# An attention encoder layer on eight cores: VectorE's chain behind each attention unit in two parts, V tiles by weight slices, the gate stage in three blocks

## What is computed

```python
a = rms_norm(h, g_mix); z = a @ w_in                     # q, k, v, u, v_gmlp
q, k = apply_partial_rope(q), apply_partial_rope(k)       # 16 of 64 dims
# differential attention, 8 heads, two softmaxes each
pr = softmax(q k^T * 64**-0.5); o = (pr[0] - lam * pr[1]) @ v
attn_out = rms_norm(o, g_subln) * (1 - lambda_init)       # per head
gmlp_out = gelu(u) * (w_spatial @ layer_norm(gelu(v_gmlp)) + b)   # chunks of 128 tokens
h = h + concat(attn_out, gmlp_out) @ w_out                # 2048 x 2048
h = h + conv_glu_ffn(rms_norm(h, g_ffn))                  # d_ff 5632, conv width 3
gate = sigmoid(rms_norm(h, g_ple) @ w_ple_gate)
h = h + (p @ w_ple_up) * gate
return rms_norm(h, g_final)
```

## Time and profile before

| | |
|---|---|
| median of 3 runs | 2027.28 us (2026.97 to 2114.86) |
| profiled execution | 2025.8 us; span of its slowest core, core 4: 2024.0 us |
| spans of the eight cores | 2012.2 to 2024.0 us |
| TensorE matmul busy | 1900.0 us, 94% |
| VectorE, ScalarE, GpSimd busy | 995.8 us (49%), 736.8 us (36%), 185.2 us (9%) |
| chain that ended last | TensorE 81%, VectorE 8%, issue 4%, ScalarE 3%, DMA 3% |
| stages of core 4, us from the start of the span | loads and K projection to 125, V to 235, attention 450 to 890, output projection's rest to 945, feed-forward to 1867, gate stage to 2009, last writes |

### The profile page before, as it was taken

One profiled execution on the slowest core, in us unless ns is written; L12 is line 12 of the kernel. 1 busy time (PEld: TensorE's weight loads), 2 busy tenths in 40 slices (PEclk: granted clock), 3 DMA queues, 4 the chain that ended last, 5 costly groups with the idle time before them and its releaser, 6 DMA issues.

```text
span 2024.0 us, 31135 instructions; the slowest of 8 cores (2012.2 to 2024.0 us)
## 1 busy us (share of the span) xinstructions
PE 1900.0 (94%) x11642; PEld 1070.0 (53%) x11710; DVE 995.8 (49%) x1305; ACT 736.8 (36%) x1018; POOL 185.2 (9%) x281
## 2 busy tenths in 40 slices
PE   5998999998898898998999999999999999999995
PEld 1443455554445555555666644666654566644442
DVE  3654231336645544453666631466641366644667
ACT  4622211107786767655222200122210122233553
POOL 5510000000000000001000000000000000001000
PEclk9998999999999989999999999999999999999997
DMA  8752054370013334456444444444444464445604
GB/s 220 220 124 52 14 93 88 51 141 29 29 57 67 69 62 82 76 98 119 74 74 80 74 74 76 83 74 75 76 73 80 77 112 74 67 74 85 109 22 146
DMA packets 62547, 170.43 MB, mean 84 GB/s; under 512 B 10944, under 2 KB 19392, under 8 KB 62272
## 3 DMA queue, kind: packets, MB, share of 16 engines
q0 software_dynamic: 34992, 125.58, 36.7%
q1 hardware_dynamic: 27152, 42.60, 6.8%
q10 hardware_dynamic: 256, 0.26, 0.0%
HBM read 279.29 MB, written 8.39 MB: 142 GB/s over the span
## 4 chain that ended last, share of the span: by engine, by line
PE 81%; DVE 8%; issue 4%; ACT 3%; DMA 3%; SPq 1%; POOL 1%; DVEq 0%; ACTq 0%; POOLq 0%
PE ps L339 81%; DVE big L345 5%; ACT big L342 3%; DMA big<-xo 1%; DVE big L357 1%; DVE big L348 1%; SPq L568 1%; DMA big<-xa 1%; POOL big L352 1%; DMA big<-wv 1%; DVEq L170 0%; DVE big L354 0%; SPq L455 0%; ACTq L170 0%; ACT L342 0%
## 5 line engine op out<-in xcount | busy, mean ns | idle before, releaser
L339 PE MATMUL ps<-big 128*128 128x342 bf16 (+3 forms) x11642 | 1900.0, 331 | 106.2 <-DVE big L345 42.2
L339 PEld LDWEIGHTS ps<-big 128*128 128x128 bf16 (+1 forms) x11710 | 1070.0, 98 | 934.7 <-issue 189.7
L342 ACT ACTIVATE big<-big 128x1024 f32<-128x1024 f32 (+10 forms) x524 | 418.6, 818 | 896.7 <-DVE big L345 706.5
L345 DVE TENSOR_TENSOR big<-big 128x342 f32<-128x342 f32 (+9 forms) x423 | 303.6, 735 | 217.0 <-ACT big L342 186.7
L342 ACT ACTIVATE big<-ps 128x684 bf16<-128x684 f32 (+1 forms) x432 | 290.5, 710 | 172.7 <-PE ps L339 164.2
L348 DVE SCALAR_TENSOR_TENSOR big<-big 128x1024 f32<-128x1024 f32 (+1 forms) x228 | 258.5, 1134 | 188.1 <-ACT big L342 175.9
L345 DVE TENSOR_TENSOR big<-ps,big 128x1026 f32<-128x1026 f32 (+4 forms) x239 | 210.7, 897 | 250.2 <-PE ps L339 236.4
L345 DVE TENSOR_TENSOR big<-big,ps 128x342 f32<-128x342 f32 (+1 forms) x96 | 82.8, 864 | 222.1 <-PE ps L339 222.1
L409 POOL DMA_DIRECT2D big<-wup x88 | 46.5, 528 | 549.2 <-PE ps L339 513.1
L342 ACT ACTIVATE big<-ps,big 128x512 bf16<-128x512 f32 x50 | 34.3, 687 | 149.5 <-PE ps L339 149.5
L409 POOL DMA_DIRECT2D big<-wo x48 | 25.5, 533 | 484.6 <-PE ps L339 476.8
(11 more groups left out here) (26 smaller groups left out, 57.0 us busy)
## 6 DMA issues: line engine op xcount, KB each, us to landing
big<-wup POOLq DMA_DIRECT2D x88, 512.0 KB, 5.0
big<-wo POOLq DMA_DIRECT2D x48, 512.0 KB, 5.5
big<-wdn POOLq DMA_DIRECT2D x32, 480.0 KB, 5.0
big<-xa SPq DMA_DIRECT2D x24, 512.0 KB, 4.8
big<-xo SPq DMA_DIRECT2D x16, 512.0 KB, 10.3
big<-wg POOLq DMA_DIRECT2D x16, 512.0 KB, 13.2
y<-big SPq DMA_DIRECT2D x32, 256.0 KB, 2.4
big<-wdn POOLq DMA_DIRECT2D x16, 448.0 KB, 4.9
```

The source lines that it names most:

```text
L339: P.op("pe", lambda e: e.matmul(out, lhsT=lhsT, rhs=rhs, start=start, stop=stop), reads=reads, writes=writes, inc=inc)
L342: P.op("act", lambda e: e.activation(out=out, in_=in_, func=func, **kw), reads=reads, writes=writes)
L345: P.op(en, lambda e: e.tensor_tensor(out=out, in0=a, in1=b, op=op), reads=reads, writes=writes)
```

## The change

**V projection.** In the first of the two calls the last four token tiles are done by weight slice: four matmuls for each of the four tiles with slice 0, then slice 1, and so on, into four banks. Each slice's slot is released as soon as its 16 matmuls are done, with an increment at the last of them.

**Start of attention.** The clearing of the padded query buffers moves before `q_mm(3)`, `q_pad(0)` before `q_mm(7)`.

**Attention units.** `post_o` loses its `split3`, which becomes `post_sq`. By step: `post_ln` 4 and 6, `post_exp` 8, `post_o` 9, `post_sq` 11, `post_b` 3 as before, but ahead of the AV matmuls and into bank 7, `post_rs` 5 and 7, `post_out` 8. `q_pad(u + 1)` goes from step 9 to 13. Spatial products stand at steps 6 and 14 of units 0 to 7. `FILL` has 32 entries for one unit: four matmuls in step 0, none in steps 1 to 4 and 10, the rest in 5 to 9 and 11 to 15; it begins at unit 9, step 5. The last two output tiles use banks 0 and 1. The loads of `h` (`h_first`, `h_last`) are spread one to a unit.

**After attention.** The remaining 32 laid-in matmuls in two groups of 16 among the post work; five `hg_copy` on ScalarE and two on VectorE, the other nine one for each tile of `wl`; the adds to `hacc2` two tiles late; `flush_sq` later.

**Gate stage.** Three blocks of 384, 384 and 256 tokens; `final` of earlier blocks through a queue `fin`, one for each tile; at the very end `emit_c` ahead of the last `emit_b`.

```diff
-        def tok_proj(items, epi, bankset, hook=None):
+        def tok_proj(items, epi, bankset, hook=None, tail=0):
...
+            for sx in range(4 if tail else 0):
+                for n, (xg, xr, t) in enumerate(items[ni:]):
+                    for kc in range(4 * sx, 4 * sx + 4):
+                        pe(ps[:, bl[n], :], xg[:, kc, t * 128:(t + 1) * 128], ws[sx][:, kc % 4, :], kc == 0, kc == 15,
+                           [sls[sx].reg] + xr(t * 128, 128, kc), [Rb[bl[n]]], kc == 15 or (n == tail - 1 and kc % 4 == 3))
+                    if sx == 3:
+                        epi(ni + n, bl[n])
+                        if hook is not None:
+                            hook()
+                release([sls[sx]])
...
-        tok_proj(vitems, v_epi(0), [6, 7, 0, 1, 2, 3], hook)
+        tok_proj(vitems, v_epi(0), [6, 7, 0, 1, 2, 3], hook, 4)
...
         for t in range(2, 8):
+            if t == 3:
+                for i in range(2):
+                    P.inherit(R_qz[i], [R_bn] + R_roth + R_RQ[2:])
+                    P.op("dve", lambda e: e.memset(qz[i], 0.0), writes=[R_qz[i]])
+            if t == 7:
+                q_pad(0)
             q_mm(t)
...
+        def post_sq(u):
             split3(RM, [R_rm], 1)
 
         def post_b(u):
-            sum3(onesb, 1)
-            tsc(RM, ps[:, 6, 0:NB], 1.0 / 128, EPS, ALU.mult, ALU.add, [Rb[6]], [R_rm])
+            sum3(onesb, 1, 7)
+            tsc(RM, ps[:, 7, 0:NB], 1.0 / 128, EPS, ALU.mult, ALU.add, [Rb[7]], [R_rm])
...
-        gen = itertools.chain(wout_gen(0, [7]), wout_gen(1, [7]))
-        FILL = [1, 1, 1, 1, 2, 1, 1, 1, 1, 1, 1, 2, 1, 1, 0, 0]
+        gen = itertools.chain(wout_gen(0, [7]), wout_gen(1, [7] * 14 + [0, 1]))
+        FILL = [2, 2] + [0] * 9 + [2, 2, 2, 2, 2, 2, 1, 2, 1, 0, 0, 2, 2, 2, 1, 1, 1, 1, 1, 1, 0]
...
-            if u < 23 and st == 9:
+            if u < 23 and st == 13:
                 q_pad(u + 1)
...
+                if st == 4:
+                    post_ln(u - 1, 0)
+                if st == 6:
+                    post_ln(u - 1, 1)
+                if st == 8:
+                    post_exp(u - 1)
+                if st == 9:
+                    post_o(u - 1)
+                if st == 11:
+                    post_sq(u - 1)
...
         def late(j, hd):
+            if len(late_add) > 1:
+                late_add.pop(0)()
...
-        for j in OJ[:6]:
+        post_sq(23)
+        for j in OJ[:5]:
             hg_copy(j)
+        for j in OJ[5:7]:
+            hg_copy(j, "dve")
...
         for n in range(6, 16):
             wl(n, 0, 16)
+            if n < 15:
+                hg_copy(OJ[n + 1])
...
+        GB = ((0, 384), (384, 384), (768, 256))
...
-                if j == 3 and bk == 1:
-                    blk_rstd(0, 7)
+                if j == 3 and bk > 0:
+                    blk_rstd(bk - 1, 7)
```

More of the change, by code:

```diff
@@ L914, in build_nc, with q_pad @@
         move(KS[s2], R_KS[s2], DS_k[s2], rope_pieces(1), NT, qT, R_qm, 0, oldx, "act")
-        for t in range(2, 8):
+        units = [(b, hh) for b in range(3) for hh in range(8)]
+        R_qz = [Reg(), Reg()]
+        def q_pad(u):
+            b, hh = units[u]
+            for c in range(2):
+                cpy(qz[u % 2][64 * c:64 * c + 64, c, :], qT[64 * c:64 * c + 64, hh, b * NB:(b + 1) * NB], R_qm[hh] + [R_qb[hh][b]],
+                    [R_qz[u % 2]])
+        for t in range(2, 8):
+            if t == 3:
[4 more added lines that the diff above has]
+                q_pad(0)
             q_mm(t)
@@ L976, in build_nc @@
         R_hacc = [Reg(), Reg()]
-        units = [(b, hh) for b in range(3) for hh in range(8)]
         LAG = 2
-        for i in range(2):
-            P.op("dve", lambda e: e.memset(qz[i], 0.0), writes=[R_qz[i]])
-        def q_pad(u):
-            b, hh = units[u]
-            for c in range(2):
-                cpy(qz[u % 2][64 * c:64 * c + 64, c, :], qT[64 * c:64 * c + 64, hh, b * NB:(b + 1) * NB], R_qm[hh] + [R_qb[hh][b]],
-                    [R_qz[u % 2]])
-        q_pad(0)
         def emit_qk(k):
@@ L1116, in build_nc @@
                 emit_qk(k)
-            fl = 9 * 16 + 8 <= k < nstep
+            fl = 9 * 16 + 5 <= k <= nstep
             if fl:
-                fill(gen, FILL[2 * st % 16])
-            if u < 9 and st in (3, 8, 12):
-                if sp_i[0] < 16:
-                    spatial_mm()
-                elif not sp_done[0]:
-                    spatial_halo()
-                    sp_done[0] = True
-                    for r in R_hacc:
-                        P.inherit(r, R_ut)
+                fill(gen, FILL[2 * st])
+            if u < 8 and st in (6, 14):
+                spatial_mm()
+            if u == 8 and st == 6:
+                spatial_halo()
+                for r in R_hacc:
+                    P.inherit(r, R_ut)
+            if 2 <= u < 24 and st == 3:
+                post_b(u - 2)
             ka = k - LAG
@@ L1241, in build_nc @@
             P.inherit(r, [R_la])
-        for j in OJ[6:]:
-            hg_copy(j)
+        flush_sq()
         for n in range(4, 6):
@@ L1249, in build_nc @@
             wl(n, 0, 16)
+            if n < 15:
+                hg_copy(OJ[n + 1])
+        while late_add:
+            late_add.pop(0)()
         R_rf = Reg("rffn")
@@ L1430, in emit_b @@
+            end = bk == NG - 1 and j == 15
+            if end:
                 act(dummy, dummy, AF.Ln, [], [R_dum])
-            tt(gt[s], ps[:, pb_, :], gt[s], ALU.mult, [Rb[pb_]], [R_gt[s]])
-            tt(hd, hd, gt[s], ALU.add, [R_gt[s]], [R_hb[bk][j]])
+                emit_c(*lastc.pop(0))
+            tt(g, ps[:, pb_, 0:n], g, ALU.mult, [Rb[pb_]], [R_gt[s]])
+            tt(hd, hd, g, ALU.add, [R_gt[s]], [R_hb[bk][j]])
             if j == 0:
-                act(hac3[:, c0:c0 + 512], hd, AF.Square, [R_hb[bk][j]], [R_hc[bk]])
+                act(hac3[:, c0:c0 + n], hd, AF.Square, [R_hb[bk][j]], [R_hc[bk]])
@@ L1439, in emit_b @@
                 emit_c(*lastc.pop(0))
-            lastc.append((bk, j))
-            if bk == 1 and j >= 3:
-                if j < 15:
-                    final(0, j - 3, "dve")
-        for bk in range(2):
-            c0 = bk * 512
+            if not end:
+                lastc.append((bk, j))
+            fin.append((bk, j))
+            if fin[0][0] < bk and (j >= 3 or fin[0][0] < bk - 1) and not end:
+                final(*fin.pop(0))
+        for bk in range(NG):
+            c0, n = GB[bk]
             for j in range(16):
```

142 lines of the change are left out of this document (73 added, 69 removed).

## The result

The changed kernel takes **1980.8 us** in the median (1980.1 to 1982.9, 4 runs). Against the runs of the kernel before on the same chip its time is 0.9773 of theirs, 95% interval [0.975, 0.9797]: faster. Forecast were 1976.0 us and a range of 1951 to 1992. In this and the following comparisons some executions of either kernel were disturbed by a lower clock on one die; they are left out, and where so many were that the median is no use, the undisturbed times are given singly.

A forecast was written before the change was run, and what follows sets the result against it. TensorE was taken as the bound almost everywhere, core 4 as slowest: 2024.0 - 19.9 - 7 - 10.3 - 4 - 9.8 - 0.5 = 1972.5; with 1.8 around the span and 1.5 to the median 1976 us, range 1951 to 1992.

The forecast's parts named there:

- V: V projection: the 8.0 us wait for second-pass weights and 2.4 us of lower clock go, -10.3 us on every core.
- A laid-in unit: Attention unit with output-projection matmuls laid in: 18.45 us forecast; fourteen of them 258.3 against 278.2, -19.9 us.
- q_pad (1.15): Laid-in attention unit: QK waits about 1.15 us for q_pad, moved behind post_o and post_sq in VectorE's queue.
- post_ln (0.4): Laid-in attention unit: a second, smaller wait, for post_ln moved from step 5 to 4, 0.4 us.
- Rival (a): Attention units: q_pad is in time, so 22 waits of 1.15 us less, 1951 us; chance 0.2.
- Rival (b): Attention units: the clock still falls in many, now at the q_pad pause; eight at 1.6 us, 1989 us; chance 0.17.
- (d): Rival, slower than before: the clock falls for two stretches in each of 23 attention units, 2050 us; chance 0.02.
- Start of attention: Between V projection and units: second step 2.7 us earlier, clock fall of about 1.3 behind the pause gone, -4 us.
- Units: Attention units: -19.9 us for fourteen with laid-in matmuls, -7 for units 0 to 9 without them.
- the 7: Units 0 to 9 without laid-in matmuls: eight take 122.4 against 128.6, one spatial product less in unit 0, -7 us.
- After attention: Stretch behind the attention units: TensorE's waits there and a clock fall of 1.7 go, -9.8 us; ends -5 and -10.
- Gate stage: Three blocks and new order at the end: +0.7 + 0.85 + 0.85 + 2.2 - 4.5 - 0.6 = -0.5 us.

## Why the prediction was right and where it was wrong

**Right in mechanism and size.** V: 10.1 of 10.3 on core 4, undone 10.4; on one core such an agreement is partly luck, since this mark lies between 442.0 and 449.6 on the eight cores before. A laid-in unit: 18.45 forecast, 18.45 measured as the average of fourteen. That both digits agree is luck, since thirteen take 18.57 and the short last one draws the average down; but the parts are right too, 1.07 for q_pad (1.15) and 0.24 for post_ln (0.4), and the clock is kept in all of them. Rival (a), q_pad in time, did not occur; brought about it is worth 21.6 us, not the 25 that I gave it, since a wait is 1.0 on average. Rival (b) did not occur, and the run with longer pauses shows how near it was: 1.2 us more a unit, and the clock falls in 9 of 23. Of (d), two falls in a unit, nothing was seen even with pauses of 3.16 us (14 falls in 15 units). The rule of the Trainium skill on idle gaps (TensorE: Matmul & The Clock Gate, "Why this matters for your kernels") holds as a direction: falls came behind pauses of 1.95, 2.2 and 3.16 us in the units and none behind 1.0. Keeping long gaps out is not enough: at the start of attention the clock fell on several cores with nothing above 1.11 us in front.

**Start of attention: the step that failed.** The term was -4: "the second step starts 2.7 us earlier, and the fall of the clock behind the pause (about 1.3) goes". Measured were 0.0 on core 4, which sets the time, and 2.2 on the mean of the cores. Both halves failed: what the earlier start won was lost again to something else that was late, and the clock fell all the same. I looked at what ended the pause of 3.50 and not at what would be late next. The moves of the last q tile leave a staging area that the seventh probability buffer covers. Their time is set by SyncE's queue: issued from 440.86, and the Exp that waits for them starts at 447.57. In the kernel before the pause hid them, no Exp waited for a transfer. Without it the seventh Exp reaches them 2.56 us too early on core 4; TensorE's pause behind it is 2.38 us there and 1.45 and 0.95 on two other cores. The other five have none; on all five the clock had fallen earlier, and the Exps came later with it. The clock was put down to the one long pause; the runs show it falling on some cores with no more than 1.11 and 0.69 in front, on none once the 1.11 was gone, and on none with the V slices undone, where all the pauses are there. What decides it stays open. The size of the term was right for what it left out: on the five cores of the run with the other buffer order that have neither the wait nor the fall, the stretch is 3.8 us shorter than on core 4 before (15.21 against 18.99). From slowest core to slowest core taking away the transfer gave 2.4 us and taking away the 1.11 another 2.3; together 4.7, where the forecast had 4 and another 0.8 for the spatial product that unit 0 has less.

**Units: the terms were too large by 5.2 us, and this is the largest part of the miss.** 1.4 of it is the base. I took 278.16 us for fourteen units between the Exps of post_exp; between the copies the same count takes 276.79, because the last unit is short (17.80) and the Exp marks cut it in half. 1.9 lie in the eight units before: they took 127.65 instead of the 128.6 of the sum and now take 123.31, 15.4 each instead of 15.3, so 4.3 gained instead of 6.2. 1.1 is the unit in which the laying-in begins, counted in the 7 with no term of its own; it became longer (17.10 to 18.22). And the 0.8 for unit 0's spatial product lies ahead of the first copy, in the stretch above.

**After attention: 11.2 instead of 9.8.** Right in its parts, against the rows above. The additional 1.4 was not taken apart. No run undoes this stage's changes, nor the new places of the spatial products; for them the account rests on the rows alone.

**Gate stage: 2.3 instead of 0.5, for reasons that partly cancel.** From restart to the last wide matmul it grew by 3.0 (127.8 against 124.8), forecast 4.6: the 2.2 for VectorE being late in the third block did not happen, the block has no pause and the wait behind it is 4.59 where it was 5.11. Core 4 has no fall there; on the five cores that have one it grew by 1.7 more. Behind the last wide matmul it won 5.3 (5.1 forecast), but that is luck, two errors that cancel: from the last wide matmul to the first of the last products it won 2.0 (9.2 us against 11.2) where 4.5 were forecast, and from there to the end 3.3 (12.1 against 15.4) where 0.6 were. The second error is this one: "SyncE's issues stand 0.62 apart over 16 writes", and "the issue is the price whatever the size", misread a row. The 0.62 of the earlier trace rows is an average. The first twelve issues follow VectorE, 0.60 apart, and only the last four stand 0.69 apart, which is SyncE's own pace with these writes; with the smaller ones it is 0.50.

Weighed against the rule of the Trainium skill (DMA: Bandwidth & Descriptors, Bandwidth), whose figure for 64 KB made 15 us an estimate for the last writes: all sixteen of 128 KB were issued and landed within 9.5 us on core 4, some 220 GB/s, and within 10.3 us on the other cores. That figure of the Trainium skill is 138 GB/s, so it was too low for this train of writes.

That the blocks of 384, 384 and 256 bring next to nothing against two of 512, I had as a sum near zero. The time agrees (0.1 us), the traces say 1.7 us less, and 2.9 where the clock stays; the sum had no term for a fall behind the restart.

**From span to median.** I added 3.3 us; here it is 2.1. So 1972.5 + 3.3 = 1976 stands against 1978.7 + 2.1 = 1980.8: the span was 6.2 off, the addition gave 1.2 back.

## What to carry to other kernels

In a program where each engine's list is its schedule, ask of each operation that moves what it now stands behind: one q_pad four steps too late cost nearly half as much as the whole change gained (21.6 of 46.5 us). The place where a bank falls free, counted in matmuls against the other engine's long chain, mattered more here than how that chain is cut. Before a stall is booked as gain, look for the transfer that it was hiding, and look at the small pauses around the place too. And when two kernels differ by 2 us in one stage, compare that stage on all cores: the slowest cores may differ by more than that before the stage begins.

## What the runs showed of the hardware that was not expected

- A fall of TensorE's granted clock (1.00 to 0.50, 2.4 to 1.2 GHz) in the attention units and behind the gate stage's restart lasts 3.4 us each time and costs 1.4 to 1.7 us. With a pause of 2.2 us in each unit it comes in every second laid-in unit on the slowest core, with 3.16 us in nearly all (14 in the attention part), with 1.0 us in none on any core. Behind the pause of 2.02 at the gate stage five of eight cores have it, behind one of 1.60 none of sixteen.
- It also comes without a pause above 1.11 us, behind 88 us of matmuls without one, and then on some cores and not on others: on three, four and five of eight in three kernels that are the same up to there. On none once the 1.11 was gone, but also on none with the V slices undone, with the 1.11 and longer pauses in place. The pauses alone don't decide it.
- Sixteen writes of 128 KB are issued 0.50 us apart from one queue and 0.34 from two, there at the pace of VectorE. The last one lands 2.0 to 2.8 us after its issue in the changed kernel, 2.9 to 3.5 with two queues.
- Between the landing of the last write and the end of the span lie 2.08 us on the cores of the profiles with one queue. SyncE's long list of waits runs inside that time, so that a shorter list would probably have bought nothing; no run tried it.
